# Two mixers of a transformer stack: delta rule before attention, output rows between heads, convolution beside the inverses

## What is computed

```python
proj = einsum('btd,de->bte', x, w_in)                       # 1024 -> 3218 columns
qkv = silu(causal_depthwise_conv(concat(a_q, a_k, a_v), w)) # 4 taps, 1152 channels
# delta rule, 6 heads of 64, chunks of 64 tokens
q = l2_normalize(q) * 64 ** -0.5; k = l2_normalize(k)
lower = where(strict, (k * beta) @ k.T * decay, 0)
t_inv = inverse(eye + lower)
u, w = t_inv @ (v * beta), t_inv @ (k * beta * exp(gc))
for i in range(4):                                           # chunks, in order
    v_new = u[i] - w[i] @ state
    o[i] = (q[i] * exp(gc[i])) @ state + a_intra[i] @ v_new
    state = state * exp(g_last) + (k[i] * exp(g_last - gc[i])).T @ v_new
o_a = rms_norm(o) * silu(gate)
# convolution of 31 taps on 256 channels
o_b = silu(layer_norm(causal_depthwise_conv(glu_a * sigmoid(glu_b), w31) + b))
# attention, 6 heads of 64, with a forget gate
o_c = softmax(causal(q @ k.T / 8 + c[t] - c[s])) @ v         # c = cumsum(log_sigmoid(f))
mix = (concat(o_a, o_b, o_c) * mix_scale) @ w_out
x = layer_norm(ALPHA * x + mix)
```

## Time and profile before

| | us |
|---|---|
| runs, median (lowest to highest of 3) | 2431.82 (2427.04 to 2434.49) |
| the profiled execution | 2426.25 |
| its span in the trace | 2424.5 |
| PE busy in it | 2299.8 (95%) |
| DVE busy | 1574.7 (65%) |
| ACT busy | 1152.0 (48%) |
| mixer of layer 0, first product to last sum | 8.14 to 231.27 |
| mixer of layer 1 | 444.17 to 662.06 |

### The profile page before, as it was taken

One profiled execution on the slowest core, in us unless ns is written; L12 is line 12 of the kernel. 1 busy time (PEld: TensorE's weight loads), 2 busy tenths in 40 slices (PEclk: granted clock), 3 DMA queues, 4 the chain that ended last, 5 costly groups with the idle time before them and its releaser, 6 DMA issues.

```text
span 2424.5 us, 31995 instructions
## 1 busy us (share of the span) xinstructions
PE 2299.8 (95%) x12173; PEld 1883.7 (78%) x12173; DVE 1574.7 (65%) x1700; ACT 1152.0 (48%) x1163; POOL 151.9 (6%) x224
## 2 busy tenths in 40 slices
PE   8887999898789999999999999999799999998998
PEld 8776888777668888888888888888588778757886
DVE  3555544456569898989898889888655318524443
ACT  1321433123147676767676767676545212223442
POOL 1010000101020000000000000000390001000000
PEclk9987999999879999999999999999899999879999
DMA  9302555440259999999999999999456454324552
GB/s 305 115 2 78 177 179 178 134 150 2 70 167 353 346 355 343 357 342 357 343 354 343 359 342 356 342 356 363 132 185 197 139 176 126 101 70 131 189 180 82
DMA packets 254772, 538.02 MB, mean 222 GB/s; under 512 B 17838, under 2 KB 146912, under 8 KB 254432
## 3 DMA queue, kind: packets, MB, share of 16 engines
q1 hardware_dynamic: 250960, 523.21, 61.7%
q0 software_dynamic: 3168, 9.86, 1.3%
q10 hardware_dynamic: 560, 3.79, 0.4%
HBM read 533.65 MB, written 3.15 MB: 221 GB/s over the span
## 4 chain that ended last, share of the span: by engine, by line
PE 92%; DVE 5%; ACT 2%; issue 1%; DMA 0%; DVEq 0%; POOL 0%; SPq 0%; ACTq 0%
PE bank L1217 9%; PE bank L1218 9%; PE bank L1221 9%; PE bank L1092 8%; PE bank L1093 8%; PE bank L1094 8%; PE bank L905 5%; PE bank L1352 5%; PE bank L1237 4%; PE bank L1232 4%; PE bank L1233 4%; PE bank L1069 3%; PE bank L901 2%; PE bank L1192 1%; PE bank L1500 1%; PE bank L1205 1%
## 5 line engine op out<-in xcount | busy, mean ns | idle before, releaser
L1984 DVE TENSOR_TENSOR weights_lo<-ring_data,weights_hi 128x2048 fp32r<-128x2048 f32 x336 | 759.2, 2289 | 98.5 <-ACT weights_hi L1715 97.3
L1715 ACT ACTIVATE weights_hi<-ring_data 128x2048 fp32r<-128x2048 f32 x336 | 636.3, 1918 | 173.7 <-DMA ring_data<-in_moe_w 173.1
L1217 PE MATMUL bank<-weights_hi,xg_hi 128*128 128x512 f32 x896 | 358.0, 400 | 4.0 <-DVE arena L2360 2.6
L1218 PE MATMUL bank<-weights_hi,xg_lo 128*128 128x512 f32 x896 | 355.4, 397 | 0.0
L1979 DVE TENSOR_TENSOR weights_lo<-ring_data,weights_hi 128x2048 fp32r<-128x2048 f32 x99 | 229.9, 2352 | 54.6 <-ACT weights_hi L1550 54.6
L1525 ACT ACTIVATE arena<-bank 128x512 f32<-128x512 f32 (+4 forms) x170 | 78.9, 483 | 359.0 <-PE bank L905 111.9
L1221 PE MATMUL bank<-weights_lo,xg_hi 128*128 128x512 f32 x896 | 242.9, 393 | 0.0
L1092 PE MATMUL bank<-weights_hi,xT_hi 128*128 128x512 f32 x528 | 213.1, 404 | 2.3 <-DVE xT_lo L1972 2.3
L1093 PE MATMUL bank<-weights_lo,xT_hi 128*128 128x512 f32 x528 | 209.4, 397 | 0.0
L1094 PE MATMUL bank<-weights_hi,xT_lo 128*128 128x512 f32 x528 | 209.3, 396 | 0.0
L1217 PEld LDWEIGHTS bank<-weights_hi,xg_hi 128*128 128x128 f32 x896 | 168.7, 188 | 43.1 <-issue 3.0
(11 more groups left out here) (434 smaller groups left out, 3275.8 us busy)
## 6 DMA issues: line engine op xcount, KB each, us to landing
ring_data<-in_moe_w SPq DMA_DIRECT2D x672, 512.0 KB, 4.3
ring_data<-in_ffn_w_in SPq DMA_DIRECT2D x88, 512.0 KB, 4.8
ring_data<-in_w_in SPq DMA_DIRECT2D x70, 512.0 KB, 4.8
ring_data<-in_ffn_w SPq DMA_DIRECT2D x66, 512.0 KB, 4.1
ring_data<-in_ffn_w_out SPq DMA_DIRECT2D x44, 512.0 KB, 4.0
ring_data<-in_w_out SPq DMA_DIRECT2D x24, 512.0 KB, 4.5
ring_data<-in_w_in SPq DMA_DIRECT2D x8, 396.0 KB, 4.3
ring_data<-in_w_in SPq DMA_DIRECT2D x8, 390.0 KB, 5.6
```

The source lines that it names most:

```text
L1217: mm(o, xg_hi[:, k, :], e_hi(at)[:, r], start=k == 0, stop=False)
L1218: mm(o, xg_lo[:, k, :], e_hi(at)[:, r], start=False, stop=False)
L1715: nc.scalar.activation(e_hi(at), ring_data[:, e_slot(at), :], ACT.Copy).then_inc(ring.hi_done, 1)
L1984: v.tensor_tensor(e_lo(at), ring_data[:, e_slot(at), :], e_hi(at), ALU.subtract).then_inc(ring.lo_done, 1)
```

## The change

All of it lies in the two mixers.

- **Order of the loads.** The attention's values and queries and the gates go to the end; the delta rule's loads and the long convolution's come first. Banks 0 and 1 alone are used for projections, and a projection can be run by halves, `project(m, g)`.
- **Delta rule first.** PE runs four loads, the sums of the decay logs, load 4 and load 5 (128 columns), the norms of queries and keys (12 products of two columns on `sq`, tokens in rows, in place of three of 512 columns), the inner products, load 6, the transposes, level 0 of the inverse, load 7 (`glua`), and then levels 1 to 5. Queries and keys are no longer normalized themselves; the factors (`norm12`, `beta1`, `beta2`, `qscale`) enter where beta and the output's norm do. ACT and DVE follow the same order.
- **Inverses.** Two groups (one per 128 tokens) in place of four. The products that update X and Y stream only the 32 columns that a level changes (`parity`), and DVE subtracts those only (`coupled`).
- **Projections between state steps.** The 12 half loads left (`fill`) stand one ahead of the first state step, two in each of three steps and one in the last; two loads stand behind the steps.
- **Convolution.** The taps are spread on DVE: two behind each of the levels 1 to 5, four more, then 6, 6 and 5 inside the first three state steps, between the new values and the state's update. The forget gate's logs stand in the third step.
- **Heads.** `scores(h)` has four products, all over 128 rows: queries lie in `fqz` with the other head's 64 rows zeroed (POOL clears them, ACT fills), and one product adds the forget sums, from the single row tile `forget`. POOL's `GF` is gone.
- **Output.** Row tiles 3, 4, 0, 1, 2 of the mixed values are turned between heads, and their output products stand between and behind the heads; tiles 5, 6, 7 (attention) follow with `last=True`.

The diff, cut to its core:

```diff
-PROJ = [(C_DECAY, 198, "tokA"), (C_FV, 195, "tokC"), (C_FV + 195, 195, "tokC")]
+PROJ = [(C_DECAY, 198, "tokA")]
...
 PROJ += [(C_GLUB, 256, "glub"), (C_GLUA, 256, "glua")]
+PROJ += [(C_FV, 195, "tokC"), (C_FV + 195, 195, "tokC"), (C_DECAY + 198, 198, "tokA")]
 PROJ += [(C_FQ + 256 * i, 256, "fqk") for i in range(3)]
-PROJ += [(C_DECAY + 198, 198, "tokA")]
+OUT_BANKS = (0, 1, 4, 5)
+CONV_PARTS = (14, 20, 26, 31)
...
-        fqk = ar(6, T)
+        fqz, fk = ar(H, T), ar(3, T)
...
+        def parity(v, n, odd):
+
+            return v.rearrange("p (b q c) -> p b q c", q=2, c=1 << n)[:, :, odd]
+
+        def coupled(j, n):
+
+            one, two = H * CHUNK, H * CHUNK + (1 << n)
+            v = arena[:, at_gm + 2 * one * j:at_gm + 2 * one * j + 2 * two].rearrange("p (w r) -> p w r", w=2)[:, :, 0:one]
+            return v.rearrange("p w (g q c) -> p w g q c", q=2, c=1 << n)[:, :, :, 0]
...
-                for j in range(TT):
-                    nc.gpsimd.tensor_tensor(GF[:, j], bc(const("gt256", j, T), 1, H), bc(gs[:, j, H:2 * H], 2, T), ALU.mult).then_inc(sem("masked_forget"), 1)
...
+                pool.wait_ge(sem("masked_logs"), 4 * (l + 1))
+                nc.gpsimd.memset(fqz[HD:P, 0:H:2, :], 0.0).then_inc(sem("decay_causal"), 1)
+                nc.gpsimd.memset(fqz[0:HD, 1:H:2, :], 0.0).then_inc(sem("decay_causal"), 1)
+                pool.wait_ge(sem("decay_causal"), 5 * l + 2)
+                nc.gpsimd.memset(forget[:, :], 0.0).then_inc(sem("decay_causal"), 1)
...
+                def project(m, g):
+
+                    c, w, kind = PROJ[m]
+                    b = m % 2
+                    if g == 0:
+                        ring.arrived(pe, n0 + m)
+                        if m - 2 == GLUA_LOAD:
                             pe.wait_ge(sem("glu_ready"), l + 1)
+                        elif m >= 2:
+                            pe.wait_ge(sem("proj_act"), act_proj(l, m - 2))
...
+                for m in range(4):
+                    project(m, 0)
+                    project(m, 1)
```

On PE, norms and scores, and the inverses' update (`half` is the mask of 64-row blocks):

```diff
-                for m in range(3):
-                    pe.wait_ge(sem("gdn_act"), 8 * l + 2 + m)
-                    pe.wait_ge(sem("qk_squares"), 3 * l + m + 1)
-                    mm(bk(5 + m, 512), half, sq[:, 2 * m:2 * m + 2, :].rearrange("p a b -> p (a b)"), start=True, stop=True).then_inc(sem("gdn_psum"), 1)
...
-                    mm(bank[b][:, 0:P], q[0], k[:, 0:P], start=True, stop=False)
-                    mm(bank[b][:, 0:P], const("le"), GF[:, 0, h, 0:P], start=False, stop=True)
-                    mm(bank[b][:, P:3 * P], q[1], k, start=True, stop=False)
-                    mm(bank[b][:, P:3 * P], ones, GF[:, 0, h, :], start=False, stop=False)
-                    mm(bank[b][:, P:3 * P], const("le"), GF[:, 1, h, :], start=False, stop=True).then_inc(sem("head_scores"), 1)
...
+                pe.wait_ge(sem("qk_squares"), 3 * (l + 1))
+                pe.wait_ge(sem("gdn_act"), 7 * l + 5)
+                for j in range(TT):
+                    for t in range(6):
+                        i = mm(bk(2, TT, 2 * H)[:, j, 2 * t:2 * t + 2], sq[:, t, P * j:P * j + P], half[:, 0:P:HD], start=True, stop=True)
+                i.then_inc(sem("gdn_psum"), 1)
...
-                                    mm(o[r, 0, t], z[r], xx[r], start=True, stop=True)
+                                    mm(o[r, 0, s], z[r], parity(xx, n, 0)[r], start=True, stop=True)
                             for c in range(2):
                                 r = half_rows(c)
-                                i = mm(o[r, 1, t], xx[r], z[r], start=True, stop=True)
+                                i = mm(o[r, 1, s], xx[r], parity(z, n, 1)[r], start=True, stop=True)
...
+                    q = [fqz[:, h, P * j:P * j + P] for j in range(TT)]
+                    k = fk[:, h // 2, :]
+                    row = ident[:, h:h + 1].broadcast_to([P, P])
+                    mm(bank[b][:, 0:P], q[0], k[:, 0:P], start=True, stop=False)
+                    mm(bank[b][:, 0:P], row, forget[:, 0:P], start=False, stop=True)
+                    mm(bank[b][:, P:3 * P], q[1], k, start=True, stop=False)
+                    mm(bank[b][:, P:3 * P], row, forget[:, :], start=False, stop=True).then_inc(sem("head_scores"), 1)
```

The filling, and the output:

```diff
+                fill = [(m, g) for m in range(GLUA_LOAD + 1, len(PROJ)) for g in range(2)]
+                project(*fill.pop(0))
...
+                    project(*fill.pop(0))
                     pe.wait_ge(sem("vnew_ready"), 2 * (4 * l + n + 1))
...
+                    if n < 3:
+                        project(*fill.pop(0))
+
+                while len(fill) > 2:
+                    project(*fill.pop(0))
+                pe.wait_ge(sem("conv_done"), l + 1)
+                pe.wait_ge(sem("state_ready"), 5 * (l + 1))
...
+                pe.wait_ge(sem("logs_ready"), 3 * l + 3)
+                pe.wait_ge(sem("o_ready"), 4 * (l + 1))
+                mm(bk(7, T)[0:H, 0:P], s1[:, 0, H:2 * H], const("le"), start=True, stop=True)
+                mm(bk(7, T)[0:H, P:T], s1[:, 0, H:2 * H], ones, start=True, stop=False)
+                mm(bk(7, T)[0:H, P:T], s1[:, 1, H:2 * H], const("le"), start=False, stop=True).then_inc(sem("gdn_psum"), 1)
+                while fill:
+                    project(*fill.pop(0))
...
+                scores(0)
+                scores(1)
+                pe.wait_ge(sem("conv_out"), l + 1)
+                turn_mixed(3, 0, 0)
+                turn_mixed(4, 0, 1).then_inc(sem("mixed_turned"), 1)
+                turn_p(0)
+                scores(2)
+                turn_p(1)
+                pe.wait_ge(sem("conv_ln"), 2 * (l + 1))
+                weigh(0)
+                pe.wait_ge(sem("mixed_ready"), l + 1)
+                turn_mixed(0, 1, 0)
+                turn_mixed(1, 1, 1).then_inc(sem("mixed_turned"), 1)
+                pe.wait_ge(sem("mixT_act"), 3 * l + 1)
+                turn_mixed(2, 0, 0).then_inc(sem("mixed_turned"), 1)
+                scores(3)
+                turn_p(2)
+                weigh(1)
+                pe.wait_ge(sem("mixT_dve"), 2 * l + 1)
+                out(0, (3, 4), first=True)
+                scores(4)
+                turn_p(3)
+                weigh(2)
+                pe.wait_ge(sem("mixT_act"), 3 * l + 2)
+                out(0, (0, 1, 2))
+                scores(5)
+                turn_p(4)
+                weigh(3)
+                out(1, (3, 4), first=True)
+                turn_p(5)
+                weigh(4)
+                out(1, (0, 1, 2))
+                weigh(5)
+                pe.wait_ge(sem("head_biased"), H * (l + 1))
+                out(2, (3, 4, 0, 1, 2), first=True)
+                out(3, (3, 4, 0, 1, 2), first=True)
                 pe.wait_ge(sem("fox_done"), l + 1)
-                pe.wait_ge(sem("o_ready"), 4 * (l + 1))
-                turn_bank(3, mixed, 3)
-                pe.wait_ge(sem("xT_act"), 2 * plain(3 * l + 1) - 1)
-                out((6, 7), first=True)
-                pe.wait_ge(sem("conv_out"), l + 1)
-                turn_bank(2, mixed, 2)
-                pe.wait_ge(sem("xT_act"), 2 * plain(3 * l + 1))
-                out((4, 5))
-                pe.wait_ge(sem("mixed_ready"), l + 1)
-                turn_bank(1, mixed, 1)
-                turn_bank(0, mixed, 0)
-                pe.wait_ge(sem("xT_dve"), 2 * plain(3 * l + 1))
-                out((2, 3, 0, 1), last=True)
+                turn_mixed(5, 6, 0)
+                turn_mixed(6, 6, 1).then_inc(sem("mixed_turned"), 1)
+                turn_mixed(7, 7, 0).then_inc(sem("mixed_turned"), 1)
+                pe.wait_ge(sem("mixT_act"), 3 * (l + 1))
+                pe.wait_ge(sem("mixT_dve"), 2 * (l + 1))
+                for m in range(OUT_LOADS):
+                    out(m, (5, 6, 7), last=True)
```

On DVE:

```diff
+                        xy = coupled(j, n)[:, w]
+                        v.tensor_tensor(xy, xy, bk(4 + j, 2, HP << (LEVELS - n), 1 << n)[:, w], ALU.subtract).then_inc(sem("inv_upd"), 1)
...
+                for n in range(1, LEVELS):
+                    level(n)
+                    long_conv(2 * n - 2, 2 * n)
 
                 v.tensor_copy(S_st[:, :, :], S_st[:, :, :]).then_inc(sem("state_ready"), 1)
+                long_conv(2 * LEVELS - 2, CONV_PARTS[0])
                 dve.wait_ge(sem("uw_act"), 4 * (l + 1))
...
+                    if n < 3:
+                        long_conv(CONV_PARTS[n], CONV_PARTS[n + 1])
+                    if n == 2:
+                        dve.wait_ge(sem("proj_act"), act_proj(l, 9))
+                        for jt in range(TT):
+                            st.do(v.scalar_tensor_tensor(s1[:, jt, 6:12], tokC[:, jt, 384:390], -1.0, hpar[:, l, 6:12], ALU.mult, ALU.subtract))
+                        softplus(1, 3).then_inc(sem("logs_ready"), 1)
                     dve.wait_ge(sem("supd_psum"), 4 * l + n + 1)
```

On ACT, behind the inverses:

```diff
+                project(8)
+                project(9)
+                softplus(1, 3)
+                project(10)
```

(8 more changed lines are left out.)

655 lines of the change are left out of this document (332 added, 323 removed).

## The result

| | before | after |
|---|---|---|
| median (lowest to highest) | 2429.43 us (2423.42 to 2434.49) | 2365.98 us (2362.36 to 2371.17) |
| span of the profiled execution | 2424.5 us | 2365.2 us |
| mixer of layer 0, first product to last sum | 223.1 us | 194.0 us |
| mixer of layer 1 | 217.9 us | 190.2 us |

Of the 59.3 us between the two spans, 56.8 lie in the mixers.

The account below looks back on a forecast made before the run. PE was taken as the bound, on the last-ending chain for 92%. Layer gains of 27.5 and 23.5 us, less 3 a layer for the clock, left 45.0: 2381, plus 5.6 for the median, 2387 us; range 2370 to 2413.

Parts of the forecast that it names:

- the first two stages: Layer 0's projections up to the first inverse level, ending at 75.0 us, then the inverses, ending at 98.9 us.
- the wait at the heads: After the last projection's copy at 153.1 us, PE waits for the convolution's norm; first weights transposed at 160.9 us.
- 3 us a layer for the lower level: Deduction from the gain for PE's 1.2 GHz clock, in the third state step and at the start of the heads.
- stage 5: Heads of layer 0, from 153.1 to 191.2 us: wait for the convolution's norm until 160.9, then 30.3 us of work.
- State steps of 9.1, 9.1, 11.1: First three state steps, in us, paced by DVE with convolution inside; the third has the forget gate's logs, 3.0.
- Five changes of mode, 1.0, and the first load, 8.3, in stage 1: Before the first inverse level: PE switching between 64-row and 128-row operands, 1.0 us; first projection load, slow start included, 8.3.
- DVE 0.6 late to the sums: End of each mixer: DVE reaches the output sums 0.6 us late, its weight splits standing just ahead of them.
- (a): State steps and heads: a third of PE's work runs at 1.2 GHz, costing 12 us a layer: 2411 us; chance 0.19.
- (b): Inverse levels: POOL's masks hold up DVE's taps, up to 1.5 us a level, 6 a layer: 2399 us; chance 0.12.
- (c): Better: 32-column inverse instructions run shorter and no clock is lost, 3 us a layer each: 2375 us; chance 0.12.
- (d): 1.2 GHz holds from first state step to last output product, some 85 us a layer: near 2530 us; chance 0.03.
- (e): Nothing moves: freed time returns as waits in state steps, three of 16 us instead of 9.1: 2430 us; chance 0.02.

Follow-up runs that it names:

- the run with three parts undone: Changed kernel without projections in the state steps, with head scores over 64 rows and output rows behind the heads: 2437.3 us, 1.0039 of the kernel before.

## Why the prediction was right or wrong

**Right.** The direction and the mechanism: projections hide in the state steps, since DVE sets their pace. The edges of the first two stages are met within 0.6 us, the second by a dip of the clock that cost what two terms had in excess (below), and so is the wait at the heads: 151.06 to 158.37 is 7.3 us, 7.8 forecast. The twelve taps (5.46 us for 12 operations, 5.5 forecast), the filling groups, the scores without the 0.63, the 0.029 for 32 columns: all as priced. These rows are DVE's timeline of one state step:

```profile
102.90 0.61 DVE L2298 TENSOR_TENSOR arena<-arena,bank 64x192 f32<-64x192 f32 x2 [0.39 <-issue]
103.44 5.46 DVE L2278 SCALAR_TENSOR_TENSOR arena<-arena,params 128x256 f32<-128x256 f32 x12
...
110.00 0.54 DVE L2313 TENSOR_TENSOR arena<-arena,bank 64x384 f32<-64x384 f32 x1
111.28 0.63 DVE L2298 TENSOR_TENSOR arena<-arena,bank 64x192 f32<-64x192 f32 x2 [0.75 <-PE bank L1034]
```

**Wrong: the size, by four terms that all err to the same side.**

- *"I take off 3 us a layer for the lower level."* In layer 0 the first trace did lose about that: 1.0 at 55.99 us (8.10 for a load that takes 7.1) and 2.5 at the heads. But it was taken off a sum whose other terms already had that much air: against the forecast of stage 5 the heads ran over by 1.6 us in layer 0 and 0.7 in layer 1, not by 3. In layer 1 there is no dip in stage 1, and 3 us of it at the heads, worth some 1.5.
- *State steps of 9.1, 9.1, 11.1.* They took 8.4, 8.8 and 9.8. I had put 1.1 us between DVE's last state operation and its next new values (0.52 for PE, 0.2 for the mode, 0.4 for hand-overs); DVE sits idle for 0.75. The new values took 0.54 in place of 0.7, the taps 5.4 in place of 5.5, and of the 3.0 for the forget gate's logs only 2.3 show. 2.3 us a layer, and 0.4 more in the last step and the first filling group.
- *Five changes of mode, 1.0, and the first load, 8.3, in stage 1.* The second trace of the changed kernel, which has no dip there, reaches the first filling group at 96.7 us, 2.2 under the forecast. Its first load takes 7.35. Layer 1 of the first trace, without a dip, takes 1.3 us less than forecast up to there.
- *DVE 0.6 late to the sums.* It wasn't; the sum begins as the product ends, at 202.3.

One term erred the other way, by less: the four levels took 18.7 us in layer 0, 18.0 forecast.

So the step that failed is the adding up: the terms were priced each with a margin, and 3 us a layer for the clock came on top. Together the mixers gave 29.1 + 27.7 us where 24.5 + 20.5 were forecast. The largest parts of that are the states (2.7 a layer) and what the heads did not use of the 3 us (1.4 and 2.3); they make 9 of the 11.8 us. These are 11.8 of the 14.3 us between the forecast of the profiled execution (45.0) and the 59.3 of the two spans. The other 2.5 are in the program outside the mixers, where executions scatter by more. The time itself was missed by 21 us: the remaining 7 are the 5.6 that I added because the median before lay above its profiled execution, while the changed kernel's lies 1.6 below. That 5.6 weighs as much as the states of both layers: without it the low end would have been 2364, and the 2366 inside. Three runs that spread over 7 us gave no ground for it; with the fourth, the median before is 2429.43.

**The rivals.** (a) the lower level persists: it does, but only when the filling is taken out (0.50 from 105 to 136 us), so filled steps were the case of the earlier trace rows's 1.00. (b) POOL: the taps are longer beside the masks, by less than the rival's 1.5 us a level, and PE doesn't notice. The changed kernel's timelines, POOL's last masks and DVE's taps beside and after them:

```profile
84.96 1.91 POOL L727 TENSOR_TENSOR arena<-arena,consts_sb 128x384 f32<-128x384 f32 x2 [3.16 <-PE bank L987]
```

```profile
84.67 2.89 DVE L2278 SCALAR_TENSOR_TENSOR arena<-arena,params 128x256 f32<-128x256 f32 x4
...
89.56 1.79 DVE L2278 SCALAR_TENSOR_TENSOR arena<-arena,params 128x256 f32<-128x256 f32 x4
```

That is 1.1 us for four operations beside 1.9 us of POOL. The Trainium skill (SBUF — State Buffer, on the shared port pair) has the two exclude each other; the lengthening agrees with it in kind, but full exclusion would have cost DVE the 1.9, and the measured 1.1 decides. (c) came nearest in time, 2375, by luck: narrow instructions save nothing, and the clock was lost still, in full in layer 0 and by half in layer 1; moving the norm got it back. (d) was never near: it needs what the run with three parts undone shows, heads and states at the lower level at once, and even there the loss was 10 us. Its 2530 doesn't follow from its own terms: 85 us a layer at up to one each would be 2557. (e) needed steps of 16 us; they took 8.4 to 9.8.

**What I should have seen.** The earlier trace rows gives 0.62 for 24 us of state steps, and I priced the kernel before by its edges alone. A mean granted clock over each mixer (0.90 and 0.92, above) would have shown some 80 us at half speed, a store from which filling gives back in all its stretches. The sum built from edges and prices at the higher level takes that gain in silently, some 20 us of lower level are left after the change, and they cost less than the 3 us a layer that looked like caution, except in layer 0.
